# Block products in pairs of token chunks and down products in pairs of output tiles, alternating PSUM banks

## The chip, the cores and the metric

One Trainium2 chip, of which one core runs the whole kernel. The metric is the device time of one execution in microseconds (us); smaller is better. Times of a kernel are medians of several executions; the trace comes from one more, profiled, execution.

## The reference

One inference step of a decoder layer for two groups of tokens that share the weights: 1024 prompt tokens and 8 x 8 sample tokens, model width 1024, all in float32. The layer is

- `x = x + 0.5 * SwiGLU_1(RMSNorm(x))`
- a combined input projection; windowed attention with three dilations (heads A) and a Conformer convolution module (channels B); `x = x + [A | B] @ W_out`
- `x = x + CrossAttention(RMSNorm(x), memory)`
- `x = x + 0.5 * SwiGLU_2(RMSNorm(x))`, and a final RMSNorm

with keys, values and convolution rows returned as new cache entries. The part that this change touches is the feed-forward half step, used twice:

```
def ffn_half_step(x, g, wg, wu, wd):
    h = rmsnorm(x, g)
    return x + 0.5 * ((jax.nn.silu(h @ wg) * (h @ wu)) @ wd)
```

`wg` and `wu` are 1024 x 2816, `wd` is 2816 x 1024. The tokens of both groups stand side by side: 1088 columns.

## The kernel before, in words

Activations are held transposed: model channels on the 128 partitions, tokens along the free dimension. A float32 product is made of three matmuls in the type fp32r: weights and activations are each split into a high and a low part, and the helper `three` (L920 to L922) issues high x high, low x high and high x low into the same PSUM bank. PSUM has eight banks, written `ps[:, bank, ...]`. The 1088 token columns are cut in two ways: into chunks of 384, 384 and 320 columns (`CHUNKS`), or into two halves of 544 (`TH`), each of two chunks of 272 (`CW`).

The hidden width 2816 is worked off in 11 groups of 256. In `ffn` of the tensor block, the first group is done plainly (`plain`): gate and up for two hidden tiles and three chunks, over 8 channel tiles each. The other ten (`REST`) are done by `halved(i)`. It replaces the eight block products of a 2 x 2 by 2 x 2 block matrix product by seven, with sums and differences of blocks as operands: for `w = 0` (gate) and `w = 1` (up) seven products `m = 0` to `6`, each over 4 channel tiles, for both 272-column chunks `c`. So one chunk of one block product is 4 x 3 = 12 matmuls. `product` (L935) issues them for one chunk; chunk 0 comes first, then chunk 1, and each has its own PSUM bank (`one + c`, `two + c` or `three_ + c`) and its own increment of the semaphore `pp`. `hh` and `hl` hold the activations' high and low parts, `th` and `tl` those of the block differences.

The weights come by DMA, issued by SP, into four quarters of `raw`. POOL makes sums and differences of blocks (L835), a high part (L803) and a low part (L805) in a ring of six slots; it waits for a slot by `pp` in steps of two or by `down` in steps of twelve.

ACT copies finished blocks out of PSUM (L1668), applies SiLU (L1673, L1688) and casts the hidden values to their high part (L1678). DVE adds a kept block to a finished one (L2311), multiplies gate and up (L2321) and makes the low part of the hidden values (L2325). The hidden values come in four pieces per group, 0 to 3, each of one hidden tile and one token half, each worked chunk by chunk. Piece 2 is finished after product 5 of `w = 1`, piece 3 after product 6. PE's waits on `up`, `part` and `hid` in `halved` say when it may write into a bank again or read the hidden values.

Then `down` (L958) multiplies the two hidden tiles by the 256 x 1024 slice of `wd`: 8 output tiles x 3 chunks = 24 tiles, six matmuls each (two hidden tiles, three parts), in four banks in turn. DVE adds half of each to `x` (L2271, `residual`) and increments `res`; PE waits before tile `j` until tile `j - 4` has been added. In the first group's `down(0, ...)` DVE makes differences of activation blocks (L2187, L2226, L2242, L2196) beside the residuals, after every fourth, and ACT casts them (L1633); both finish them before their part of `halved(0)`. In the last group of the second feed-forward the tiles go by rows of tokens, `beside_down` transposes finished tokens on PE (L1589) between them, and DVE writes the normalised output (L2820) beside the residuals.

Every engine follows its own list, written out by hand; nothing reorders it.

## Time and profile before

| | |
|---|---|
| time, median of 3 | 2586.61 us (2585.22 to 2592.68) |
| time of the profiled execution | 2590.64 us |
| its span | 2588.6 us |
| mean granted clock of TensorE | 0.99 |
| PE busy | 2487.2 us, 96% |
| PE weight loads busy | 2335.2 us, 90% |
| DVE busy | 1226.5 us, 47% |
| POOL busy | 1160.4 us, 45% |
| ACT busy | 662.6 us, 26% |
| data moved | 224.67 MB, 87 GB/s |

The span is the profiler's, from the first to the last instruction; the time of the execution has 2.0 us around it. PE is TensorE. Its matmuls are pipelined and each is shown longer than the distance to the next one, so the distance between the starts of two matmuls says what one costs. PEld are the weight loads, which run beside the matmuls. What stands in brackets, as `[0.49 <-PE ps L922]`, is the time in which the engine had nothing to run before this row, and what ended it.

### The profile page before, as it was taken

The page shows a single profiled execution, that of the slowest core. Times are in us where ns is not written, and L with a number is a line of the kernel's source. Part 1 is how long each engine was busy: PE and PEld are TensorE (multiplying, and loading weights), DVE is VectorE, ACT ScalarE, POOL GpSimd, SP SyncE. Part 2 cuts the span into 40 slices and gives each one's busy share as a digit, 9 for nine tenths or more (in the row PEclk, how much of TensorE's full clock was granted, in tenths as well). Part 3 has the DMA queues.
Part 4 walks back from the last instruction along what each step waited for, and adds up shares of the span by engine and source line. Part 5 has one row for each costly group of instructions (what it writes and reads, how often), then busy time and mean ns, then how long its engine had stood idle before and what let it go on. Part 6 is the DMA issues. An engine that isn't in the chain of part 4 may idle for free.

```text
span 2588.6 us, 48515 instructions
## 1 busy us (share of the span) xinstructions
PE 2487.2 (96%) x17731; PEld 2335.2 (90%) x17731; DVE 1226.5 (47%) x2562; ACT 662.6 (26%) x1673; POOL 1160.4 (45%) x1068
## 2 busy tenths in 40 slices
PE   7999999999999999989999999889899999999997
PEld 7999999999998899967557999669799999999997
DVE  5653333333335799544433342642963333333335
ACT  4321111111113224266223122331321111111113
POOL 7466666666664222023001220213166666666662
PEclk9999999999999999999999999999999999999999
DMA  7311111111112112155864123641011111111112
GB/s 236 96 42 47 46 46 46 46 46 47 49 49 73 33 53 88 72 161 163 334 245 154 49 76 118 260 173 50 17 46 45 48 45 47 45 46 46 48 49 94
DMA packets 215993, 224.67 MB, mean 87 GB/s; under 512 B 12090, under 2 KB 183670, under 8 KB 211795
## 3 DMA queue, kind: packets, MB, share of 16 engines
q1 hardware_dynamic: 199399, 195.46, 23.3%
q10 hardware_dynamic: 16492, 27.82, 2.9%
q8 instruction: 68, 1.11, 0.2%
q14 instruction: 34, 0.28, 0.0%
HBM read 190.84 MB, written 32.40 MB: 86 GB/s over the span
## 4 chain that ended last, share of the span: by engine, by line
PE 88%; DVE 6%; ACT 2%; DMA 2%; issue 1%; ACTq 0%; DVEq 0%; SPq 0%
PE ps L920 25%; PE ps L921 25%; PE ps L922 25%; PE ps L1427 1%; PE ps L1383 1%; PE ps L1397 1%; PE ps L1302 1%; PE ps L1315 1%; DMA cK<-in_cache_mem_k 1%; PE ps L1493 1%; DVE ps L2187 1%; PE ps L1476 1%; DVE ps L2407 1%; PE ps L1285 1%; DVE hl L2384 0%
## 5 line engine op out<-in xcount | busy, mean ns | idle before, releaser
L920 PE MATMUL ps<-hh,wh 128*128 128x272 f32 (+2 forms) x2528 | 781.8, 309 | 21.0 <-ACT gated L1639 7.0
L921 PE MATMUL ps<-hh,wl 128*128 128x272 f32 (+2 forms) x2528 | 778.3, 308 | 0.0
L922 PE MATMUL ps<-hl,wh 128*128 128x272 f32 (+2 forms) x2528 | 778.1, 308 | 0.0
L805 POOL TENSOR_TENSOR wl<-raw,wh 128x512 fp32r<-128x512 f32 x384 | 496.7, 1293 | 30.8
L920 PEld LDWEIGHTS ps<-hh,wh 128*128 128x128 f32 x2528 | 477.8, 189 | 32.1 <-DVE hl L2152 9.0
L921 PEld LDWEIGHTS ps<-hh,wl 128*128 128x128 f32 x2528 | 477.2, 189 | 0.5
L922 PEld LDWEIGHTS ps<-hl,wh 128*128 128x128 f32 x2528 | 476.6, 189 | 0.0
L803 POOL CAST wh<-raw 128x512 fp32r<-128x512 f32 x384 | 236.1, 615 | 532.1 <-PE ps L922 462.5
L2271 DVE SCALAR_TENSOR_TENSOR x<-ps,x 128x384 f32<-128x384 f32 (+1 forms) x528 | 280.1, 535 | 200.4 <-PE ps L922 198.2
L795 POOL CAST wh<-raw 128x1024 fp32r<-128x1024 f32 x52 | 54.1, 1040 | 701.6 <-PE ps L922 576.0
L920 PE MATMUL ps<-hidh,wh 128*128 128x384 f32 (+1 forms) x1056 | 344.6, 326 | 1.2 <-DVE tl L2196 1.2
L922 PE MATMUL ps<-hidl,wh 128*128 128x384 f32 (+1 forms) x1056 | 344.5, 326 | 0.0
L921 PE MATMUL ps<-hidh,wl 128*128 128x384 f32 (+1 forms) x1056 | 344.1, 326 | 0.0
L920 PE MATMUL ps<-th,wh 128*128 128x272 f32 x960 | 276.3, 288 | 3.0 <-ACT gated L1668 3.0
L921 PE MATMUL ps<-th,wl 128*128 128x272 f32 x960 | 277.2, 289 | 0.0
L922 PE MATMUL ps<-tl,wh 128*128 128x272 f32 x960 | 275.9, 287 | 0.0
L835 POOL TENSOR_TENSOR raw<-raw 128x512 f32<-128x512 f32 x160 | 206.9, 1293 | 0.0
L920 PEld LDWEIGHTS ps<-hidh,wh 128*128 128x128 f32 x1056 | 198.3, 188 | 1.7 <-DVE tl L2196 1.5
L2311 DVE TENSOR_TENSOR ps<-ps,parts 128x272 f32<-128x272 f32 x120 | 53.8, 448 | 306.4 <-PE ps L922 306.4
L921 PEld LDWEIGHTS ps<-hidh,wl 128*128 128x128 f32 x1056 | 198.2, 188 | 0.0
L922 PEld LDWEIGHTS ps<-hidl,wh 128*128 128x128 f32 x1056 | 198.2, 188 | 0.0
L2311 DVE TENSOR_TENSOR gated<-ps,gated 128x272 f32<-128x272 f32 x120 | 53.0, 442 | 300.5 <-PE ps L922 300.5
(274 smaller groups left out, 3320.7 us busy)
## 6 DMA issues: line engine op xcount, KB each, us to landing
raw<-in_ffn_gate SPq DMA_DIRECT2D x88, 256.0 KB, 2.9
raw<-in_ffn_up SPq DMA_DIRECT2D x88, 256.0 KB, 2.9
raw<-in_ffn_down SPq DMA_DIRECT2D x88, 256.0 KB, 2.7
Kw<-in_cache_win_k SPq DMA_DIRECT2D x24, 512.0 KB, 6.1
Vw<-in_cache_win_v SPq DMA_DIRECT2D x24, 512.0 KB
raw<-in_w_in SPq DMA_DIRECT2D x20, 512.0 KB, 3.8
Kw<-in_cache_win_k SPq DMA_DIRECT2D x8, 1024.0 KB, 8.5
Vw<-in_cache_win_v SPq DMA_DIRECT2D x8, 1024.0 KB
```

What stands on the lines that cost most here:

```text
L795: pool.tensor_copy(hi, src).then_inc(w_hi, 1)
L803: pool.tensor_copy(ring_hi(r), quadrant(q)).then_inc(s["whi"], 1)
L805: pool.tensor_tensor(ring_lo(r), quadrant(q), ring_hi(r).bitcast(F32), ALU.subtract).then_inc(s["lo"], 1)
L835: pool.tensor_tensor(out, a, b, op).then_inc(s["mix"], 1)
L920: pe.matmul(out, w_hi_, a_hi, start=first, stop=False, skip_group_check=more)
L921: pe.matmul(out, w_lo_, a_hi, start=False, stop=False, skip_group_check=more)
L922: return pe.matmul(out, w_hi_, a_lo, start=False, stop=last, skip_group_check=more)
L1285: mm = pe.matmul(ps[:, 2 * h + n % 2, far(t):far(t) + near(t)], qs[64 * h:64 * h + 64, 1 - p, t * P:(t + 1) * P], kTp[64 * h:64 * h + 64, ...
L1302: mm = pe.transpose(ps[0:w, b, k * P:(k + 1) * P], Sb[:, n % 2, h, c:c + w], ident[:])
L1315: mm = pe.matmul(ps[:, 6 + n % 2, 64 * h:64 * h + 64], PT[:, n % 2, h, len(cuts) + k, :], vtok[:, p, t + 1 - len(whole) + k, 64 * h:64 * h ...
L2271: dve.scalar_tensor_tensor(out=x[:, d, c0:c0 + n], in0=ps[:, bank(j), 0:n], scalar=0.5, in1=x[:, d, c0:c0 + n], op0=ALU.mult, op1=ALU.add) ...
L2311: dve.tensor_tensor(out(c), ps[:, bank + c, 0:CW], kept(c), ALU.add).then_inc(s["part"], 1)
```

## The change

`product` is taken out. In its place `pair` issues one block product for both chunks: for each channel tile and each of the three parts (high x high, low x high, high x low) first the matmul of chunk 0 into one bank, then that of chunk 1 into the next bank, with the same weights. Both chunks then end with consecutive matmuls, and each still increments `pp`. The waits for chunk 0 and for chunk 1 become one wait for both, ahead of the product. In `down` two output tiles of the same chunk are taken together: their matmuls alternate between the two tiles' banks, with different weights and the same activations, and PE waits ahead of a pair until both banks are free. The number of matmuls, the operands of each, the order in which semaphores are incremented and the lists of the other engines stay as they are.

```diff
--- before.py
+++ after.py
@@ -932,12 +932,6 @@
         def ffn(s, sn, beside_last=None):
             lo, sg, hid, res = s.base["lo"], s.base["sg"], s.base["hid"], s.base["res"]
 
-            def product(out, r, k0, k1, a_hi, a_lo, first, last, more=False):
-                for k in range(k0, k1):
-                    mm = three(out, ring_hi(r)[:, k - k0], ring_lo(r)[:, k - k0], a_hi(k), a_lo(k), first and k == k0,
-                               last and k == k1 - 1, more)
-                return mm
-
             def plain(w, c, f):
                 c0, n = CHUNKS[c]
                 j = 6 * w + 2 * c + f
@@ -956,7 +950,7 @@
                 mm.then_inc(s["gate"], 1)
 
             def down(it, lo_need, hid_need, bank, by_rows, beside=None):
-                for j in range(NC * KT):
+                for j in range(0, NC * KT, 2):
                     if by_rows:
                         c, d = divmod(j, KT)
                     else:
@@ -966,19 +960,37 @@
                         pe.wait_ge(s["lo"], lo_need(d // 4))
                     if d % 4 == 0 and (by_rows or d == 0):
                         pe.wait_ge(s["hid"], hid_need(c))
-                    pe.wait_ge(s["res"], it * (NC * KT) + (res + j + 1))
+                    pe.wait_ge(s["res"], it * (NC * KT) + (res + j + 2))
                     if beside is not None and j == 2:
                         pe.wait_ge(s["hid"], hid_need(NC - 1))
                     for f in range(2):
                         r = 2 + 2 * (d // 4) + f
-                        mm = three(ps[:, bank(j), 0:n], ring_hi(r)[:, d % 4], ring_lo(r)[:, d % 4],
-                                   hidh[:, f, c0:c0 + n], hidl[:, f, c0:c0 + n], f == 0, f == 1)
-                    mm.then_inc(s["down"], 1)
+                        for q, (w_, a_) in enumerate(((ring_hi(r), hidh), (ring_lo(r), hidh), (ring_hi(r), hidl))):
+                            for e in range(2):
+                                mm = pe.matmul(ps[:, bank(j + e), 0:n], w_[:, (d + e) % 4], a_[:, f, c0:c0 + n],
+                                               start=f == 0 and q == 0, stop=f == 1 and q == 2)
+                                if f == 1 and q == 2:
+                                    mm.then_inc(s["down"], 1)
                     if beside is not None:
-                        beside(c, d)
+                        for e in range(2):
+                            beside(c, d + e)
+
+            def pair(first_bank, r, k0, src_hi, src_lo, at, first, more):
+
+                for k in range(k0, k0 + KT // 2):
+                    whi, wlo = ring_hi(r)[:, k - k0], ring_lo(r)[:, k - k0]
+                    kk = k if src_hi is hh else k - k0
+                    start, stop = first and k == k0, k == k0 + KT // 2 - 1
+                    for part_, (w_, a_) in enumerate(((whi, src_hi), (wlo, src_hi), (whi, src_lo))):
+                        for c in range(2):
+                            mm = pe.matmul(ps[:, first_bank + c, 0:CW], w_, a_[:, kk, at + c * CW:at + (c + 1) * CW],
+                                           start=start and part_ == 0, stop=stop and part_ == 2,
+                                           skip_group_check=more)
+                            if stop and part_ == 2:
+                                mm.then_inc(s["pp"], 1)
 
             def halved(i, beside=None):
-                pp, cp, ad = s.base["pp"] + 28, s.base["up"], s.base["part"]
+                cp, ad = s.base["up"], s.base["part"]
                 for w in range(2):
                     one, two, three_ = ((0, 2, 4), (6, 4, 2))[w]
                     for m in range(7):
@@ -988,41 +1000,30 @@
                             pe.wait_ge(s["rstd"], s.base["rstd"] + (24 if m == 1 else 32))
                         if w == 0 and m == 1:
                             pe.wait_ge(s["res"], i * (NC * KT) + (res + 4 + NC * KT))
-                        for c in range(2):
-                            if w == 1 and m == 1:
-                                pe.wait_ge(s["part"], i * 12 + (ad + c + 1))
-                            if w == 1 and m == 3:
-                                pe.wait_ge(s["part"], i * 12 + (ad + 4 + c + 1))
-                            if m == 2:
-                                pe.wait_ge(s["up"], i * 12 + (cp + 6 * w + c + 1))
-                            if m == 4:
-                                pe.wait_ge(s["up"], i * 12 + (cp + 6 * w + 4 + c + 1))
-                            if m == 6:
-                                pe.wait_ge(s["part"], i * 12 + (ad + 6 * w + 2 + c + 1))
-                            x0, x1 = c * CW, (c + 1) * CW
-                            y0, y1 = TH + x0, TH + x1
-                            if m == 0:
-                                mm = product(ps[:, one + c, 0:CW], n % RING, 0, 4, lambda k: hh[:, k, x0:x1],
-                                             lambda k: hl[:, k, x0:x1], True, True)
-                            elif m == 1:
-                                mm = product(ps[:, three_ + c, 0:CW], n % RING, 0, 4, lambda k: th[:, 0, k, x0:x1],
-                                             lambda k: tl[:, 0, k, x0:x1], True, True)
-                            elif m == 2:
-                                mm = product(ps[:, one + c, 0:CW], n % RING, 0, 4, lambda k: th[:, 1, k, x0:x1],
-                                             lambda k: tl[:, 1, k, x0:x1], False, True, True)
-                            elif m == 3:
-                                mm = product(ps[:, two + c, 0:CW], n % RING, 4, 8, lambda k: hh[:, k, x0:x1],
-                                             lambda k: hl[:, k, x0:x1], True, True)
-                            elif m == 4:
-                                mm = product(ps[:, one + c, 0:CW], n % RING, 0, 4, lambda k: hh[:, k, y0:y1],
-                                             lambda k: hl[:, k, y0:y1], False, True, True)
-                            elif m == 5:
-                                mm = product(ps[:, three_ + c, 0:CW], n % RING, 0, 4, lambda k: th[:, 2, k, x0:x1],
-                                             lambda k: tl[:, 2, k, x0:x1], False, True, True)
-                            else:
-                                mm = product(ps[:, one + c, 0:CW], n % RING, 4, 8, lambda k: hh[:, k, y0:y1],
-                                             lambda k: hl[:, k, y0:y1], False, True, True)
-                            mm.then_inc(s["pp"], 1)
+                        if w == 1 and m == 1:
+                            pe.wait_ge(s["part"], i * 12 + (ad + 2))
+                        if w == 1 and m == 3:
+                            pe.wait_ge(s["part"], i * 12 + (ad + 6))
+                        if m == 2:
+                            pe.wait_ge(s["up"], i * 12 + (cp + 6 * w + 2))
+                        if m == 4:
+                            pe.wait_ge(s["up"], i * 12 + (cp + 6 * w + 6))
+                        if m == 6:
+                            pe.wait_ge(s["part"], i * 12 + (ad + 6 * w + 4))
+                        if m == 0:
+                            pair(one, n % RING, 0, hh, hl, 0, True, False)
+                        elif m == 1:
+                            pair(three_, n % RING, 0, th[:, 0], tl[:, 0], 0, True, False)
+                        elif m == 2:
+                            pair(one, n % RING, 0, th[:, 1], tl[:, 1], 0, False, True)
+                        elif m == 3:
+                            pair(two, n % RING, 4, hh, hl, 0, True, False)
+                        elif m == 4:
+                            pair(one, n % RING, 0, hh, hl, TH, False, True)
+                        elif m == 5:
+                            pair(three_, n % RING, 0, th[:, 2], tl[:, 2], 0, False, True)
+                        else:
+                            pair(one, n % RING, 4, hh, hl, TH, False, True)
                 down(i + 1, lambda h: i * NS + (lo + NP + 16 + 2 * h if beside is None else lo + NP + 18),
                      lambda c: i * 8 + (hid + 6 + (6 if c == 0 else 8)),
                      (lambda j: 4 + j % 4) if beside is not None else (lambda j: (4, 5, 2, 3)[j % 4]),
```

## Rows read from the trace of the kernel before

**Rows 1.** The page: busy time by engine; the last chain by line.

```profile
PE 2487.2 (96%) x17731; PEld 2335.2 (90%) x17731; DVE 1226.5 (47%) x2562; ACT 662.6 (26%) x1673; POOL 1160.4 (45%) x1068
...
PE ps L920 25%; PE ps L921 25%; PE ps L922 25%; PE ps L1427 1%; PE ps L1383 1%; PE ps L1397 1%; PE ps L1302 1%; PE ps L1315 1%; DMA cK<-in_cache_mem_k 1%; PE ps L1493 1%; DVE ps L2187 1%; PE ps L1476 1%; DVE ps L2407 1%; PE ps L1285 1%; DVE hl L2384 0%
```

**Rows 2.** A steady stretch: PE busy (matmuls), granted clock, DMA share, GB/s.

```profile
1929.00:1994.00 65.00, 65.00 (x475) 1.00 0.17 49
```

**Rows 3.** Groups by shape, PE: names, shapes, count | busy us, mean ns | idle.

```profile
L920 PE MATMUL ps<-hh,wh 128*128 128x272 f32 x1280 | 367.5, 287 | 0.0
...
L920 PE MATMUL ps<-th,wh 128*128 128x272 f32 x960 | 276.3, 288 | 3.0 <-ACT gated L1668 3.0
...
L920 PE MATMUL ps<-hidh,wh 128*128 128x384 f32 x704 | 235.8, 335 | 1.2 <-DVE tl L2196 1.2
```

**Rows 4.** Timeline of DVE, steady down product: start us, duration us.

```profile
2029.84 0.56 DVE L2271 SCALAR_TENSOR_TENSOR x<-ps,x 128x384 f32<-128x384 f32 x1 [0.58 <-PE ps L922]
...
2037.12 0.56 DVE L2271 SCALAR_TENSOR_TENSOR x<-ps,x 128x384 f32<-128x384 f32 x1 [0.48 <-PE ps L922]
```

**Rows 5.** Timeline of PE: the last down tile, and the next block product's first matmul.

```profile
2039.55 0.31 PE L920 MATMUL ps<-hidh,wh 128*128 128x320 f32 x1
...
2040.43 0.29 PE L920 MATMUL ps<-hh,wh 128*128 128x272 f32 x1
```

**Rows 6.** Timeline of PE: first matmuls of four successive block products (one chunk each).

```profile
2050.98 0.29 PE L920 MATMUL ps<-hh,wh 128*128 128x272 f32 x1
...
2052.49 0.29 PE L920 MATMUL ps<-hh,wh 128*128 128x272 f32 x1
...
2054.01 0.28 PE L920 MATMUL ps<-hh,wh 128*128 128x272 f32 x1
...
2055.49 0.28 PE L920 MATMUL ps<-th,wh 128*128 128x272 f32 x1
```

**Rows 7.** Timeline of DVE: the same sum in two successive groups.

```profile
2006.60 0.45 DVE L2311 TENSOR_TENSOR ps<-ps,parts 128x272 f32<-128x272 f32 x1 [13.10 <-PE ps L922]
...
2072.44 0.45 DVE L2311 TENSOR_TENSOR ps<-ps,parts 128x272 f32<-128x272 f32 x1 [13.10 <-PE ps L922]
```

**Rows 8.** Timeline of DVE in W_out: residuals of successive 384-column products of 24 matmuls.

```profile
1454.86 0.56 DVE L2368 TENSOR_TENSOR x<-ps,x 128x384 f32<-128x384 f32 x1 [2.60 <-PE ps L922]
...
1459.02 0.56 DVE L2368 TENSOR_TENSOR x<-ps,x 128x384 f32<-128x384 f32 x1 [3.20 <-PE ps L922]
```

**Rows 9.** Line L1225: count, min/median/max ns, first to last start us.

```profile
L1225 PEld LDWEIGHTS ps<-ya,ones x24: 187/190/190, 1063.4 to 1070.3; 128*128 128x128 f32 x24
```

**Rows 10.** Timeline of DVE and PE from the last block products to down.

```profile
2014.12 0.45 DVE L2311 TENSOR_TENSOR ps<-ps,parts 128x272 f32<-128x272 f32 x1 [0.49 <-PE ps L922]
2014.48 0.79 DVE L2321 TENSOR_TENSOR ps<-ps,gated 128x272 f32<-128x272 f32 x2
2015.37 0.79 DVE L2325 TENSOR_TENSOR hidl<-ps,hidh 128x272 fp32r<-128x272 f32 x2
...
2016.71 0.33 PE L920 MATMUL ps<-hidh,wh 128*128 128x384 f32 x1
```

**Rows 11.** Timeline of DVE and PE in the first down product.

```profile
1886.65 1.94 DVE L2271 SCALAR_TENSOR_TENSOR x<-ps,x 128x384 f32<-128x384 f32 x4
...
1887.35 0.41 PE L920 MATMUL ps<-hidh,wh 128*128 128x384 f32 x1
...
1890.11 1.48 DVE L2271 SCALAR_TENSOR_TENSOR x<-ps,x 128x384 f32<-128x384 f32 x3
...
1906.98 0.29 PE L920 MATMUL ps<-hh,wh 128*128 128x272 f32 x1
```

**Rows 12.** Timeline of ACT and PE at the first group of `halved`.

```profile
1914.22 1.26 ACT L1668 COPY gated<-ps 128x272 f32<-128x272 f32 x4
...
1914.66 0.39 PE L920 MATMUL ps<-th,wh 128*128 128x272 f32 x1 [1.48 <-ACT gated L1668]
```

**Rows 13.** Timeline of DVE: the last residuals of the kernel.

```profile
2569.53 1.02 DVE L2271 SCALAR_TENSOR_TENSOR x<-ps,x 128x320 f32<-128x320 f32 x2
```

## The prediction

> **What bounds the kernel now.** The page comes first: PE is busy 96% of the span, the others at most 47%, and the chain that ended last spends three quarters of the span on the three lines of `three` [rows 1]. The granted clock is 1.00 in the feed-forward stages [rows 2]. So the first reading is TensorE, at its higher level (2.4 GHz). Busy PE doesn't say why each matmul takes what it takes, so the groups by shape give the counts [rows 3], and the order of time gives the distance from one start to the next, which is the real price. Down tiles of six 384-column matmuls follow each other at 1.04 us (2029.84 to 2037.12, seven tiles in 7.28 us) [rows 4], 173.3 ns a matmul; a tile of six 320-column ones takes 0.88 us (2039.55 to 2040.43), 146.7 ns [rows 5]. The difference, 26.6 ns for 64 columns, is 0.416 ns a column; what is left is a fixed part of 13.3 ns a matmul. Block products of twelve 272-column matmuls take 1.48 to 1.52 us, on average (2055.49 - 2050.98) / 36 = 125.3 ns [rows 6]: 113.2 ns of columns and 12.1 ns fixed. Steady blocks repeat every 65.84 us (2006.60 to 2072.44) [rows 7]; 336 x 125.3 ns + 96 x 173.3 ns + 48 x 146.7 ns = 65.8 us. Nothing is left for stalls. DVE, ACT and POOL wait for PE there, not PE for them.
>
> So the change can gain only from the fixed part, and can lose wherever the new order makes PE wait.
>
> **Part 1: the bank alternates from matmul to matmul.** It touches 6720 block matmuls (2 feed-forwards, 10 repeats, 336: the 960 + 1280 of one line, times three) and 3168 down matmuls ((704 with 384 columns and, for the third chunk, half as many with 320) x 3) [rows 3]. Count, columns and arithmetic stay. If the fixed part were the price of two consecutive matmuls into one bank, one gap without it would stand at each bank switch that exists today. A down product switches after 6 matmuls, a W_out product after 24, with the same 384 columns. The 24 take 1459.02 - 1454.86 = 4.16 us, 173.3 ns each [rows 8]; the 6 take 1.04 us, 173.3 ns each [rows 4]. A saving of 13.3 ns per switch would make the average of the short product 1.7 ns smaller (13.3 x (1/6 - 1/24)), 10 ns a tile, 0.07 us over the seven tiles. They show nothing of it. What the 272-column products do vary with is the columns read: the second half's last chunk takes 1.48 us (2054.01 to 2055.49), the first half's second chunk 1.51 (2050.98 to 2052.49) and the second half's first 1.52 (2052.49 to 2054.01) [rows 6]. That points to the reading side. I take 0 for this part. The bounds: all 6720 products of a pair at the best of these rates (1.48/12 = 123.3 ns) give -15 us, at the worst (1.52/12 = 126.7 ns) +8 us, since the alternating chunks change the sequence of addresses; and if the whole fixed part went, 6720 x 12.1 + 3168 x 13.3 ns = -123 us.
>
> The Trainium skill ("TensorE: Matmul & The Clock Gate", Back-to-back issue gap) gives N/2.4 + 2.5 ns for a warm matmul. This trace disagrees: 173.3 ns stands where the rule has 162.5, and 125.3 where it has 115.8. Were the new order to restore the rule, an estimate by that page is 6720 x 9.5 + 3168 x 10.8 ns, some 98 us less; it lies inside the rival below, which is worked out from rows.
>
> **Part 2: same weights twice in succession.** In `pair` both chunks use one weight tile before the next. Today's totals have 17731 loads for 17731 matmuls, and the LayerNorm sums, whose stationary operand is `ones` throughout, have 24 loads for 24 passes [rows 1, 9]. So I expect 17731 loads again, and 0. The bound, if half the block loads vanished with their fixed part, is 3360 x 12.1 ns = -41 us.
>
> **Part 3: both chunks end together.** The evacuation of chunk 0 used to run under chunk 1's 1.5 us. Now both finish 0.125 us apart, and the next user of the bank has one product pair (3.01 us) left instead of 4.5. Copies and sums are short: two ACT copies at 0.31 us pitch [rows 12] or two DVE sums at 0.36 us (2014.12 to 2014.48 [rows 10]). The tightest case is hidden piece 2, which down waits for. Now: the last matmul of product 5 is over when DVE adds at 2014.12, then two multiplies (2014.48), two ACT casts, two subtractions (2015.37 with 0.79), end 2016.16; down's first matmul starts at 2016.71 [rows 10]. A wake-up takes 0.14 us (residual 0 starts at 1886.65 and takes 0.56 us, so it is over at 1887.21; PE starts at 1887.35 [rows 11]), so the margin is 0.41 us. Afterwards the sum of chunk 0 comes 0.125 us ahead of 2014.12 and that of chunk 1 0.36 us behind it; multiplies at 2014.72 instead of 2014.48: +0.24 us. Margin 0.17 us, no stall. The other case, +0.36 us per extra DVE start with no overlap of the casts (another 0.39 us), would be 0.75 us, and is a rival. POOL and SP are not touched: their waits count complete pairs (`pp` in twos, `down` in twelves), which are reached at the same moment.
>
> **Part 4: down in pairs.** A pair needs the residuals of the pair two back. In the repeats DVE takes 0.56 us a tile against 1.04 us of PE [rows 4]: 2.08 us for a pair against 1.04 of DVE, no stall. Not so in the first down product, where DVE first finishes other work and then makes differences beside the residuals. Residual 0 starts at 1886.65, and PE's tile 4 starts right behind its end, at 1887.35 [rows 11]. I stepped through the 24 tiles with 1.04 and 0.88 us a tile on PE, 0.48 and 0.44 us pitch for a residual, and other DVE work after every fourth: 1.6 us the first time (1888.59 to 1890.11 [rows 11]), 1.85 later, once 2.25. One by one, this ends at 1906.84; the trace has the next product's first matmul at 1906.98 [rows 11]. In pairs, PE waits 0.57 us at tile 4 (for residual 1), 0.34 at tile 12 and 0.19 at tile 20, and DVE's last difference comes 1.15 us later. That chain goes on through ACT: its first block copies start at 1914.22 behind the last cast, and PE waits 1.48 us for the first [rows 12]. Now PE needs two, 0.31 us apart (1.26 / 4). So +1.46 us per feed-forward, +2.9 us for both. Bounds: 0 (a shorter DVE list) and twice that.
>
> At the end of the first feed-forward the norm waits for the last residual, now behind one more: +0.3 us. In the last down product, which runs beside the output transposes, DVE has residuals and outputs without a gap, and its last residuals run from 2569.53 to 2570.55 [rows 13]; pair (2,0), (2,1) gives it its first tile 0.88 us later, and the output of token tile 0 stands between residuals that come in twos. Stepped through, the last residual ends near 2571.6 instead of 2570.55: +1.1 us, all of it in the tail.
>
> The Trainium skill ("Perfetto Trace Analysis", Matmuls) has independent groups rotate through banks so that one group's evacuation overlaps the next group's matmuls; pairing halves that rotation. By that rule this change costs overlap; the rows above price it at the 4 us of the sum.
>
> **Sum.** 0 + 0 + 0 + 2.9 + 0.3 + 1.1 = +4.3 us. The profiled execution took 2590.64 us (span 2588.6 and 2.0 around it), 4.0 above the median of 2586.61. On it the sum is 2595; on the median, which is what will be compared, 2591. Without the rivals its range is 2585 to 2598.
>
> **Rivals.** (1) *The fixed part goes or shrinks with alternation or with repeated weights.* For it: it is the only thing in the matmul stream above the column rate. Against it: the rows under part 1. Whole: 2591 - 123 = 2468; with repeated weights alone: 2550. Chance 0.12.
> (2) *Reading order.* The new sequence of moving addresses shifts the 272-column gap within its seen spread. For it: 1.48 against 1.52 us for identical work. To 2576 at best, 2599 at worst; chance 0.07 for a gain that counts and 0.06 for a loss.
> (3) *Evacuation becomes the bound, slower.* One mechanism: the chain of hidden piece 2, in each of 20 blocks. It decides when it grows by more than 0.41 us. If the second chunk's cast and subtraction don't overlap (0.75 us), each block stalls 0.34 us, 7 us in all, and the multiplies of piece 3 push the first residuals too; 2598 to 2602. For it: margin only 0.17 us after my own sum. Against it: casts and multiplies overlap in the rows of now. Chance 0.15.
> The forecast as summed: 0.60, of which some 0.03 lies beyond +0.3%.
>
> **How the numbers follow.** A change within 0.3% (7.8 us) is what a measurement of this kernel can't tell from none; it is said once. Faster: rival 1 and the better half of 2, 0.12 + 0.07, and 0.01 of the forecast for the unforeseen: 0.20. Slower: 0.06 + 0.15 + 0.03 = 0.24, less 0.02 where rival 3 stays under 7.8 us: 0.22. Same: 0.58. The range, 2576 to 2602, leaves out rival 1 and a little at either end.
>
> **What would show it.** Gap between starts of block matmuls: 125 to 126 ns if right, near 115 if rival 1. Loads still 17731. Sum, multiply and cast of both chunks close together, and down's first matmul without idle time in front; idle there in each block is rival 3. In the first down product, idle before the third pair, near 0.6 us. If the time falls by more than 1%, the step that failed is part 1 or 2; if it rises by more than 0.5%, part 3.

## The result, and the profile after

Fifteen executions of each kernel on one chip: before 2588.82 us (2585.22 to 2603.21), after 2594.30 us (2588.36 to 2599.46). The ratio is 1.0023, with a 95% interval of 1.0014 to 1.0033: the change costs 5.9 us (3.6 to 8.5). The forecast was +4.3 us, within 0.3%; the direction and the place were right, two of the terms were not. The profiled execution of after took 2591.56 us with a span of 2589.4, only 0.8 us more than the span of before. That is not the difference to explain: one execution differs from the next by several us in stages that the change doesn't touch (below), so the stretches around the change are compared one by one.

Lines of the page of after: the engines; the chain by engine; the costliest groups (block products, down product, the block products that read differences, and weight loads), with the names, shapes and count, then busy us, mean ns and idle time ahead with what ended most of it.

```profile
PE 2490.9 (96%) x17731; PEld 2339.3 (90%) x17731; DVE 1192.4 (46%) x2562; ACT 642.6 (25%) x1673; POOL 1159.0 (45%) x1068
...
PE 89%; DVE 6%; ACT 2%; issue 1%; DMA 1%; ACTq 0%; DVEq 0%; SPq 0%
...
L986 PE MATMUL ps<-hh,wh 128*128 128x272 f32 x1280 | 264.9, 288 | 0.0
...
L970 PE MATMUL ps<-hidh,wh 128*128 128x384 f32 (+1 forms) x1056 | 259.5, 326 | 0.4 <-DVE x L2272 0.4
...
L986 PE MATMUL ps<-th,wh 128*128 128x272 f32 x960 | 200.2, 290 | 3.6 <-ACT gated L1669 3.6
...
L986 PEld LDWEIGHTS ps<-hh,wh 128*128 128x128 f32 x1280 | 202.1, 188 | 0.0
```

PE is still the chain and has as many loads as before [rows 1]: 17731. The reader is to see two things that are not as they were. The loads of the line that now uses each weight tile twice in a row are still 1280, one for each matmul. And the idle time in front of the block products has gone from 3.0 us [rows 3] to 3.6 us, all of it behind ACT's copies.

Next the steady groups, in the timeline of DVE and then of PE. Columns are start, duration, engine, line, operation, and in brackets the idle time ahead and what ended it; x2 or x4 at the end are so many instructions drawn as one.

```profile
2007.80 0.80 DVE L2312 TENSOR_TENSOR ps<-ps,parts 128x272 f32<-128x272 f32 x2 [14.29 <-PE ps L986]
...
2013.81 0.80 DVE L2312 TENSOR_TENSOR ps<-ps,parts 128x272 f32<-128x272 f32 x2 [0.44 <-PE ps L986]
2014.52 0.79 DVE L2322 TENSOR_TENSOR ps<-ps,gated 128x272 f32<-128x272 f32 x2
2015.40 0.79 DVE L2326 TENSOR_TENSOR hidl<-ps,hidh 128x272 fp32r<-128x272 f32 x2
...
2020.73 1.02 DVE L2272 SCALAR_TENSOR_TENSOR x<-ps,x 128x384 f32<-128x384 f32 x2 [1.06 <-PE ps L970]
2022.81 1.02 DVE L2272 SCALAR_TENSOR_TENSOR x<-ps,x 128x384 f32<-128x384 f32 x2 [1.06 <-PE ps L970]
...
2073.67 0.80 DVE L2312 TENSOR_TENSOR ps<-ps,parts 128x272 f32<-128x272 f32 x2 [14.29 <-PE ps L986]
```

```profile
2016.29 0.41 PE L986 MATMUL ps<-hl,wh 128*128 128x272 f32 x2
2016.53 0.52 PE L970 MATMUL ps<-hidh,wh 128*128 128x384 f32 x2
```

The period is 65.87 us (2007.80 to 2073.67) where it was 65.84 [rows 7]. Hidden piece 2 runs through its sum, multiply and low part in the same way as before [rows 10]: from the first sum to the end of the low part 2.38 us now (2013.81 to 2016.19). Down's first matmul starts at 2016.53, 0.34 us after that end and 0.24 us behind the start of the last block pair, which is the distance of one pair, so there is no idle time. A pair of down tiles takes 2.08 us (2020.73 to 2022.81), twice the 1.04 of [rows 4]. So in 18 of the 20 groups nothing waits, and the loss must lie at the ends.

The table gives the distances between the starts of the first matmuls of neighbouring stretches in the profiled executions ("tail" runs to the end of the last instruction):

```
us                              before    after    difference
feed-forward 1: first down       23.72    23.91    +0.19
                first group      43.88    45.76    +1.88
                nine groups     592.62   592.86    +0.24   (9 x 65.847, 9 x 65.873)
                last down        24.51    24.75    +0.24
feed-forward 2: first down       24.03    24.70    +0.67
                first group      43.88    45.78    +1.90
                nine groups     592.62   592.89    +0.27
                tail             45.11    45.87    +0.76
sum                                               +6.15
not touched: before PE's first
             matmul             13.61    12.91    -0.70
             from it to the
             first down        123.58   121.50    -2.08
             attention, mixing 1061.03  1058.48    -2.55
```

"First group" is the 336 block matmuls of the first `halved`, without its down product; "nine groups" start with that down product and end where the last one starts. The sum, +6.15, agrees with the +5.9 that was timed. The last two of the untouched stretches took 121.5 to 123.6 us and 1057.9 to 1063.9 us over all the kernels below, in no relation to their edits, and that hides the difference between single spans.

3.8 of the 6.15 us lie in the two first groups. Here is the second of them, in the timelines of ACT and PE of after:

```profile
1911.88 0.39 ACT L1634 CAST hh<-ps 128x272 fp32r<-128x272 f32 x1 [2.31 <-DVE ps L2243]
1912.16 1.26 ACT L1669 COPY gated<-ps 128x272 f32<-128x272 f32 x4
```

```profile
1912.90 0.52 PE L986 MATMUL ps<-th,wh 128*128 128x272 f32 x2 [1.82 <-ACT gated L1669]
...
1914.01 0.61 PE L986 MATMUL ps<-th,wl 128*128 128x272 f32 x2
...
1914.88 0.66 PE L986 MATMUL ps<-th,wh 128*128 128x272 f32 x2
...
1916.69 0.66 PE L986 MATMUL ps<-th,wl 128*128 128x272 f32 x2
...
1917.54 0.41 PE L986 MATMUL ps<-hh,wh 128*128 128x272 f32 x2
1917.79 0.41 PE L986 MATMUL ps<-hh,wl 128*128 128x272 f32 x2
```

Before, PE started 0.44 us behind ACT's first copy (1914.22 and 1914.66 [rows 12]); now it needs two copies and starts 0.74 us behind it (1912.16 and 1912.90), and its idle time is 1.82 us, where it was 1.48. That step is the forecast's. What it didn't foresee comes 1.1 us later: from 1914.01 to 1917.54 eight pairs take 3.53 us, 0.44 each, and then a pair takes 0.25 again. The windows of PE say why; columns are the stretch, its length, PE busy with the matmuls, the granted clock, the DMA share and GB/s.

```profile
1915.00:1917.00 2.00, 2.00 (x11) 0.50 0.02 6
...
1919.00:1921.00 2.00, 2.00 (x18) 1.00 0.00 0
```

The granted clock is 0.50 there, the lower of TensorE's two levels (1.2 GHz), after it had been 1.00 up to the wait, and a matmul of 272 columns takes 0.226 us (eight in the 1.81 us from 1914.88 to 1916.69). Eight pairs cost 3.53 - 8 x 0.251 = 1.5 us more. In the first feed-forward of the same execution it is the same:

```profile
164.00:168.00 4.00, 2.18 (x12) 0.80 0.55 158
168.00:172.00 4.00, 4.00 (x28) 0.77 0.12 37
172.00:176.00 4.00, 4.00 (x34) 1.00 0.00 0
```

In the kernel before the windows around the same waits all have 1.00, as this one, which holds the second:

```profile
1912.00:1916.00 4.00, 2.52 (x20) 1.00 0.46 133
```

The timeline of PE in the first down product of the second feed-forward shows the paired wait on the residuals:

```profile
1885.03 0.59 PE L970 MATMUL ps<-hidh,wh 128*128 128x384 f32 x2 [0.39 <-DVE x L2272]
...
1892.51 0.46 PE L970 MATMUL ps<-hidl,wh 128*128 128x320 f32 x2
1892.95 0.58 PE L970 MATMUL ps<-hidh,wh 128*128 128x384 f32 x2
```

At tile 4 the wait is shown; at tile 12 it is to be read from the starts: 0.44 us behind the pair ahead, where a pair of 320 columns takes 0.29.

At the end of the kernel the last residuals are late. These are the first matmuls of the last down product, of before and of after, and DVE's last residuals of after:

```profile
2543.49 0.33 PE L920 MATMUL ps<-hidh,wh 128*128 128x384 f32 x1
```

```profile
2543.55 0.58 PE L970 MATMUL ps<-hidh,wh 128*128 128x384 f32 x2
```

```profile
2570.47 0.89 DVE L2272 SCALAR_TENSOR_TENSOR x<-ps,x 128x320 f32<-128x320 f32 x2
```

The last residual ends 27.81 us behind the start of the last down product (2571.36 - 2543.55); before it was 27.06 (2570.55 [rows 13] - 2543.49): +0.75, which is the tail's +0.76.

### The profile page after: what moved, and what is told of

It is laid out like the page before. It is cut to its first block, busy times and chain, and to the rows that moved or that the text cites. A ratio compares the mean times of both kernels' runs of the same rounds, so it can differ in the third digit from the quotient of the medians.

```text
span 2589.4 us, 48155 instructions
## 1 busy us (share of the span) xinstructions
PE 2490.9 (96%) x17731; PEld 2339.3 (90%) x17731; DVE 1192.4 (46%) x2562; ACT 642.6 (25%) x1673; POOL 1159.0 (45%) x1068
## 4 chain that ended last, share of the span: by engine, by line
PE 89%; DVE 6%; ACT 2%; issue 1%; DMA 1%; ACTq 0%; DVEq 0%; SPq 0%
PE ps L986 32%; PE ps L970 20%; PE ps L920 8%; PE ps L922 7%; PE ps L921 7%; PE ps L1384 2%; PE ps L1428 1%; PE ps L1398 1%; PE ps L1303 1%; PE ps L1316 1%; DMA cK<-in_cache_mem_k 1%; PE ps L1494 1%; PE ps L1477 1%; DVE ps L2188 1%; DVE ps L2408 1%
## 5 line engine op out<-in xcount | busy, mean ns | idle before, releaser
L920 PE MATMUL ps<-hh,wh 128*128 128x384 f32 (+1 forms) x1248 | 414.8, 332 | 19.4 <-ACT gated L1640 7.1
L922 PE MATMUL ps<-hl,wh 128*128 128x384 f32 (+1 forms) x1248 | 410.1, 329 | 0.0
L921 PE MATMUL ps<-hh,wl 128*128 128x384 f32 (+1 forms) x1248 | 409.8, 328 | 0.0
L986 PE MATMUL ps<-hh,wl 128*128 128x272 f32 x1280 | 264.9, 288 | 0.0
L986 PE MATMUL ps<-hh,wh 128*128 128x272 f32 x1280 | 264.9, 288 | 0.0
L986 PE MATMUL ps<-hl,wh 128*128 128x272 f32 x1280 | 264.6, 288 | 0.0
L970 PE MATMUL ps<-hidh,wh 128*128 128x384 f32 (+1 forms) x1056 | 259.5, 326 | 0.4 <-DVE x L2272 0.4
L970 PE MATMUL ps<-hidh,wl 128*128 128x384 f32 (+1 forms) x1056 | 259.3, 326 | 0.0
L970 PE MATMUL ps<-hidl,wh 128*128 128x384 f32 (+1 forms) x1056 | 259.0, 326 | 0.0
L986 PE MATMUL ps<-th,wl 128*128 128x272 f32 x960 | 199.6, 289 | 0.0
```

Of the source, the lines that this page charges most:

```text
L920: pe.matmul(out, w_hi_, a_hi, start=first, stop=False, skip_group_check=more)
L921: pe.matmul(out, w_lo_, a_hi, start=False, stop=False, skip_group_check=more)
L922: return pe.matmul(out, w_hi_, a_lo, start=False, stop=last, skip_group_check=more)
L970: mm = pe.matmul(ps[:, bank(j + e), 0:n], w_[:, (d + e) % 4], a_[:, f, c0:c0 + n], start=f == 0 and q == 0, stop=f == 1 and q == 2)
L986: mm = pe.matmul(ps[:, first_bank + c, 0:CW], w_, a_[:, kk, at + c * CW:at + (c + 1) * CW], start=start and part_ == 0, stop=stop and part ...
```

## Experiments

The theory of the start: the loss comes from the first down product and the first group, where the residuals and the copies decide when PE goes on, and half of it is the clock that falls behind the longer wait (this half came with the profiles of e1 to e4; the expectations count with it from e8 on). Its rival is a cost spread over all groups: alternating banks, repeated weights, or the order in which the moving operand is read. All ratios are against the kernel before in the same comparison (2586.68 us, 30 runs, for the first four; 2587.25 us, 23 runs, for the others).

### Either half of the change alone

`e1_blocks_paired` keeps `pair` and takes `down` back:

```diff
-                for j in range(0, NC * KT, 2):
+                for j in range(NC * KT):
...
-                    pe.wait_ge(s["res"], it * (NC * KT) + (res + j + 2))
+                    pe.wait_ge(s["res"], it * (NC * KT) + (res + j + 1))
...
-                        for q, (w_, a_) in enumerate(((ring_hi(r), hidh), (ring_lo(r), hidh), (ring_hi(r), hidl))):
+                        mm = three(ps[:, bank(j), 0:n], ring_hi(r)[:, d % 4], ring_lo(r)[:, d % 4],
+                                   hidh[:, f, c0:c0 + n], hidl[:, f, c0:c0 + n], f == 0, f == 1)
```

> Block products in pairs, down tiles one by one as before. Theory A (the alternating order itself costs nothing; the change loses only where PE waits longer): DVE's list in the first down product is not delayed, so only the second ACT copy (0.31 us, twice) and the 0.04 us a steady group that the changed kernel's block products took more (42.17 against 42.13 us, 18 groups) remain: +1.4 us over before, about 4 us below the changed kernel. Rival B (what the change costs is spread evenly over the reordered matmuls): 6720 of 9888 of them are here, so two thirds of the 5.9 us, +4. Rival C (chunks that finish together make PE wait in each group): +3 or more, with idle time of PE before down in each group.

`e2_down_paired` is the kernel before with only the new `down` (the same lines the other way round).

> Down tiles in pairs, block products chunk by chunk as before. Theory A: PE waits at tiles 4, 12 and 20 of the first down product, DVE's differences come 1.1 us later and with them the first group's third block product (1.1 to 1.6 us, twice); +0.2 us at the end of the first feed-forward, +0.7 us in the last down product; steady down products 23.70 instead of 23.72 us: +3 to +4 us over before. Rival B (spread evenly): 3168 of 9888, one third, +2 us.

Measured: e1 2593.09 us (8 runs), ratio 1.0020 [1.0009, 1.0030]; e2 2591.55 us (11), 1.0020 [1.0009, 1.0030]. By time the two can't be told from each other or from the whole change, so the stretches have to do it (differences to before, us):

```
                     first down   first group    nine groups    last down   tail    sum
e1_blocks_paired     0.00, 0.00   +1.86, +0.32   +0.24, +0.27   -0.02       +0.78   +3.5
e2_down_paired      +0.22, +0.68  +0.05, +0.04    0.00, 0.00    +0.25       +1.44   +2.7
after               +0.19, +0.67  +1.88, +1.90   +0.24, +0.27   +0.24       +0.76   +6.15
```

The first down product belongs to the paired `down` alone, the nine groups and the first group to the paired blocks alone. And the two first groups of e1 show the two parts of the latter apart. They wait alike, but only one of them is followed by a lower clock. First the timeline of PE in e1, in the first and in the second feed-forward, then its windows behind the first wait and behind the second:

```profile
167.53 0.52 PE L982 MATMUL ps<-th,wh 128*128 128x272 f32 x2 [1.78 <-ACT gated L1665]
```

```profile
1917.68 0.52 PE L982 MATMUL ps<-th,wh 128*128 128x272 f32 x2 [1.77 <-ACT gated L1665]
```

```profile
168.00:172.00 4.00, 4.00 (x22) 0.57 0.24 66
172.00:176.00 4.00, 4.00 (x34) 1.00 0.00 0
```

```profile
1920.00:1924.00 4.00, 4.00 (x34) 1.00 0.00 0
```

So the second copy costs 0.3 us, and the clock 1.5 us when it falls. The expectation for e1 counted only the former and was too low for that reason. Its time alone, +5.2 us (2.3 to 7.8), would fit the +4 of rival B, the evenly spread cost, as well; the stretches refute that rival, since the 18 steady groups together hold 0.5 us. For e2 +3 to +4 us were expected. The stretches give +2.7, of which 0.7 is the lower clock in the tail (below): the two first down products cost 0.2 and 0.7 us where 1.1 to 1.6 each stood.

The tails need one more look, because e1 has the old `down` there and still loses 0.78 us. The last 32 transposes of the kernel, by the timelines of PE, first after, then e1, then e2:

```profile
2575.58 3.68 PE L1590 MATMUL ps<-ident,x 128*128 128x128 f32 x32 [0.97 <-DVE ytok L2821]
```

```profile
2578.13 5.29 PE L1586 MATMUL ps<-ident,x 128*128 128x128 f32 x32 [0.97 <-DVE ytok L2817]
```

```profile
2578.57 6.62 PE L1593 MATMUL ps<-ident,x 128*128 128x128 f32 x32 [0.97 <-DVE ytok L2824]
```

And the window of PE in e2 that the last of them lies in:

```profile
2580.00:2584.00 4.00, 4.00 (x21) 0.50 0.47 190
```

The longer ones are again the lower clock, behind the short waits on DVE between the transposes; before, after, e5, e6 and e7 have 3.7 us for the same work, e3, e4 and e8 5.1 to 5.4. It comes and goes between executions, in one of four with an unpaired last `down` and in four of six with a paired one, too few to say whether the pairing has a part in it. The tail's price of the paired `down` is therefore read from the executions without it: +0.76 (after) and +0.79 (e6). The start of these 32 transposes, which the clock behind them can't move, says the same: it comes 31.2 to 31.3 us behind the start of the last down product in before, e1, e5 and e7, and 32.0 to 32.1 us in the six kernels with the paired one.

### The first down product and the first group as before, the rest paired

```diff
-            down(0, lambda h: lo + 10 + 2 * h, lambda c: hid + 2 * c + 2, lambda j: 4 + j % 4, False)
+            down_single(0, lambda h: lo + 10 + 2 * h, lambda c: hid + 2 * c + 2, lambda j: 4 + j % 4, False)
+            halved_single(0)
             if beside_last is None:
-                with pe.Fori(0, REST) as i:
+                with pe.Fori(1, REST) as i:
                     halved(i)
```

`down_single` and `halved_single` are the old functions, the latter with a paired down product behind its block products.

> The changed kernel, but the first down product and the block products of the first halved group are one by one as before, in both feed-forwards. Theory A: the waits of the first group go back to before (first halved group 43.88 us instead of 45.76, first down product without the added waits); left are 17 or 18 steady groups at +0.03 us and the last down products, +1.0 us: +1.5 us over before, 4 to 4.5 below the changed kernel. Rival B: 9 tenths of the reordered matmuls are still there, +5.3 us, no more than 0.6 us below the changed kernel.

Measured: 2592.23 us (11 runs), ratio 1.0017 [1.0008, 1.0026]. By the stretches: first down 0.00 and -0.03, first group +0.07 and +0.06, nine groups +0.25 and +0.28, last down +0.24, tail +1.48 (with the lower clock, its 32 transposes took 5.06 us), sum +2.4. Expected were +1.5 over before; without the tail's lower clock (0.7 us) 1.6 of the 2.35 are left. The loss at the start is gone, as the theory of the start has it, and the nine groups are unchanged at 65.873 us each, so nothing of the 3.8 us was spread over groups. The time itself fell less than the stretches say (+4.4 us, interval 2.1 to 6.7, against +2.4): by the ratios e3 is 1.5 us below the whole change, where 4 to 4.5 were expected and rival B allowed 0.6. The interval holds both, and this run's time alone would not have decided.

### The weight tiles of chunk 1 in another order

```diff
-                    for part_, (w_, a_) in enumerate(((whi, src_hi), (wlo, src_hi), (whi, src_lo))):
+                    parts_ = ((whi, src_hi), (wlo, src_hi), (whi, src_lo))
+                    for part_ in range(3):
                         for c in range(2):
+                            w_, a_ = parts_[(0, 1, 2)[part_] if c == 0 else (1, 0, 2)[part_]] if part_ < 2 else parts_[2]
```

For the first two parts chunk 1 takes them in the other order; banks still alternate with every matmul. The six matmuls of a channel tile now load high, low, low, high, high, high, where after has high, high, low, low, high, high. So the expectation below is right that only one pair in three has the same weights in both chunks, but a weight tile still comes directly after itself in three of six cases, as often as in after. This run is no test of repeated weights.

> The changed kernel, but in each block product the two chunks use different weight tiles (high and low in turn) for the first four of six matmuls, so the banks still alternate while only one pair in three repeats its weights; the same sums in another order. Theory A: neither the bank nor a repeated weight tile has a part in the gap between matmuls: 125 to 126 ns a block matmul, 17731 weight loads, time as the changed kernel within 2 us. Rival D (alternation costs what repetition gives back, the two cancel): the gap grows by some ns, 6720 x 2 ns = 13 us for each 2 ns.

Measured: 2593.02 us (10 runs), ratio 1.0025 [1.0016, 1.0035], the same as the whole change, and each of the eight stretches but the tail is within 0.03 us of after's. Its page, and the window behind the wait of the second feed-forward:

```profile
PE 2493.0 (96%) x17731; PEld 2343.4 (90%) x17731; DVE 1192.4 (46%) x2562; ACT 643.3 (25%) x1673; POOL 1160.6 (45%) x1068
```

```profile
1915.00:1917.00 2.00, 2.00 (x11) 0.50 0.44 127
```

Which chunk reads which weight tile makes no difference, and the clock falls here too, in both first groups. What separates the bank from the repeated weights is the down product. Its paired form alternates banks and never repeats a weight tile, and from its first matmul to the next block product the steady stretch of 144 matmuls takes 23.718 us in e2 and 23.717 in before, and 23.704 in both after and e1, whose `down` is unpaired. So alternation alone costs nothing; the 0.013 us go with the paired block products on either side. Repeated weights are in the block products of e6 and not in those of e5, next.

### The start column of the moving operand

The nine groups lose 0.026 us each. The kernel before reads 272-column chunks that start at columns 0, 272, 544 and 816 (in the block differences at 0 and 272). To separate the start column from the order, `e5_starts_single` (from before) and `e6_starts_paired` (from after) use chosen starts, with the same remainder by 64 for both chunks. The `32 * (k % 2)` keeps the remainder the same for all channel tiles of the block differences, whose rows of 544 columns are 32 more than a multiple of 64. Both kernels so read other columns than the layer needs, and the values of their feed-forwards are not the layer's; the matmuls, their sizes and all waits stay. The edit as it stands in e6 (in e5 `product` gets the same starts):

```diff
+            def start_of(w, m, c, k):
+                ph = ((0, 0, 16, 16, 32, 32, 48), (8, 48, 8, 24, 40, 24, 56))[w][m]
+                if m in (1, 2, 5):
+                    return 128 * c + (ph + 32 * (k % 2)) % 64
+                return 256 * c + (448 if m in (4, 6) else 0) + ph
...
-                            mm = pe.matmul(ps[:, first_bank + c, 0:CW], w_, a_[:, kk, at + c * CW:at + (c + 1) * CW],
+                            x0 = start_of(w, m, c, k)
+                            mm = pe.matmul(ps[:, first_bank + c, 0:CW], w_, a_[:, kk, x0:x0 + CW],
```

> The kernel before, with the moving operands of the block products read from other columns than they should be (so the feed-forward's values are others; nothing else is left out): each product starts at a chosen column, with a remainder by 64 of 0, 16, 32, 48 in the gate products and of 8, 24, 40, 56 in the up products, the same for both chunks and all channel tiles. Theory A (the 12 ns above the column rate and their spread come from the reading of the moving operand): the gap follows the start column, 123 to 127 ns by remainder, whichever bank is written. Rival: it doesn't follow it, and all 14 products show 125 to 126 ns or keep the pattern of before.

> The same start columns in the changed kernel (same remark on the values). Theory A: with equal remainders in both chunks the paired products show the same gap as the chunk-wise ones with that remainder, within 0.5 ns, since neither bank nor repeated weights matter. Rival (the pairing itself adds something per matmul): they are slower at every remainder by a like amount, 0.5 ns or more.

Measured, one execution each: 2584.84 and 2596.07 us. Single executions can't be compared as times; the distances within them can. The groups (timeline of DVE, the sum of rows 7, first e5, then e6) have one period, 65.81 us:

```profile
2001.10 0.45 DVE L2316 TENSOR_TENSOR ps<-ps,parts 128x272 f32<-128x272 f32 x1 [13.02 <-PE ps L922]
...
2066.91 0.45 DVE L2316 TENSOR_TENSOR ps<-ps,parts 128x272 f32<-128x272 f32 x1 [13.02 <-PE ps L922]
```

```profile
2012.86 0.80 DVE L2319 TENSOR_TENSOR ps<-ps,parts 128x272 f32<-128x272 f32 x2 [14.19 <-PE ps L993]
...
2078.67 0.80 DVE L2319 TENSOR_TENSOR ps<-ps,parts 128x272 f32<-128x272 f32 x2 [14.19 <-PE ps L993]
```

The mean distance from matmul to matmul within a block product, as the median over the groups (first start of a product to first start of the next, by 24):

```
ns, w = 0        m0      m1      m2      m3      m4      m5      m6
before         125.79  125.58  125.29  125.79  124.88  125.46  124.83
after          126.08  125.50  125.29  126.46  125.12  125.00  125.00
e5 (single)    125.17  125.25  126.67  126.67  126.62  126.67  123.50
e6 (paired)    125.17  125.25  126.67  126.67  126.62  126.67  123.50
```

e5 and e6 agree to the last digit in all seven, and as exactly in the seven of `w = 1`. So with equal remainders alternating banks and using one weight tile twice together change nothing, and as alternation alone changes nothing in `down`, neither does the repeated weight tile. One matmul of 272 columns takes 123.4 to 126.7 ns by where it starts: 125.2 at remainder 0, 126.7 at 16 and 32, 123.5 at 40 and 48. That is the spread; the 10 to 13.5 ns above the 113.2 ns of columns are there at every remainder tried, and no run shows what they are. After differs from before because its chunks start 272 columns apart, remainder 16, and the two are now read in turn: m3 +0.67, m0 +0.29, m5 -0.46. Over the 336 matmuls that is +0.04 us; the stretch of the down product gives 0.01 back (23.717 to 23.704), and +0.026 is left. The sum, 0.51 us in 18 groups, is small but is the whole of the steady loss.

e6 is again a case in which the clock fell behind one of its two long waits: first group +0.33 and +1.83 us. Over the eight kernels that have the wait:

```
idle time of PE before the third block product     first groups   clock fell behind it
1.48 to 1.57 us  (before, e2, e3, e5)                    8               0
1.77 to 1.85 us  (after, e1, e4, e6)                     8               6
```

In e1 the two waits are equal (1.78 and 1.77 us) and the clock fell behind one of them only, so the length alone doesn't decide. The Trainium skill ("TensorE: Matmul & The Clock Gate", Part 1) calls the number of slow matmuls at a start variable from run to run of one kernel. What varied here is whether the clock fell; where it did, the number of slow matmuls was 15 or 16 each of the six times.

### Taking away the wait

The wait of the first group is for ACT, whose copies of block product 0 stand in its list behind its last casts of block differences, though they need none of them. `e7_copy_first_before` (from before) and `e8_copy_first_after` (from after) move the copies ahead of the last two casts, in the first group alone:

```diff
-            for q in range(24, 32):
-                turned(q)
-
-            def halved(i):
+            def halved(i, first=False):
...
+                    for q in range(24, 30):
+                        turned(q)
+                    keep(0, 0, gated, 0)
+                    for q in range(30, 32):
+                        turned(q)
...
-            with act.Fori(0, REST) as i:
+            halved(0, True)
+            with act.Fori(1, REST) as i:
```

> The kernel before; ACT makes the first group's first block copies ahead of its last two casts of differences instead of behind them. Theory A: PE's wait at the third block product (1.5 us by the list of waits, a gap of 1.77 us) is for those copies only, so it goes, in both feed-forwards: first group 42.2 instead of 43.9 us, 3 us less in all, if the sixth and seventh block products don't wait then. Rival: the last differences (needed by the fourth product) are late next, and 1 us or less is won.

> The same move of ACT's copies in the changed kernel. Theory A: the changed kernel loses in its first groups by a wait of 2.1 us instead of 1.77 and by the half clock that follows it (some 15 matmuls at 227 ns instead of 125, 1.5 us); without the wait there is no half clock, both first groups take 42.2 us instead of 45.8, 7 us less than the changed kernel and 1 us or so below before. Rival (the half clock comes from the pairing or from chance, not from that wait): matmuls at 227 ns remain in one or both first groups and at most 4 us are won.

Measured: e7 2586.14 us (11 runs), ratio 0.9993 [0.9984, 1.0002]; e8 2588.28 us (12 runs), ratio 1.0003 [0.9994, 1.0011]. The timeline of ACT and the windows of PE in e8, first feed-forward:

```profile
164.42 0.68 ACT L1666 COPY gated<-ps 128x272 f32<-128x272 f32 x2 [0.41 <-PE ps L986]
165.63 0.39 ACT L1634 CAST hh<-ps 128x272 fp32r<-128x272 f32 x1 [0.54 <-DVE ps L2248]
```

```profile
164.00:168.00 4.00, 4.00 (x35) 1.00 0.44 123
168.00:172.00 4.00, 4.00 (x34) 1.00 0.48 141
```

PE doesn't wait and the clock stays at 1.00. The first groups take 42.17 us in e8 and 42.13 in e7, against 45.8 in after and 43.88 in before: 3.6 us less in each feed-forward of the one and 1.75 in the other. Of the change's 0.23%, 0.03% is left, with an interval that holds 1. But before has the wait too, and loses 1.75 us by it, so e8 against before mixes two changes. The price of pairing without the wait is e8 against e7: +2.85 us by the stretches (0.4 of it the lower clock in the tail of e8) and 0.10%, some 2.6 us, by the two ratios, where it is 6.15 and 5.9 us with the wait. This is the test of the largest term: with the wait both of its prices go, the 0.3 us and the 1.5 us of clock. For e7 the stretches say -3.5 us and the timing -1.8 (-4.1 to +0.5); no gain over the kernel before can be claimed from these runs. For e8 1 us or so below before was expected; the stretches say -0.7 and the timing +0.8 (-1.6 to +2.8).

## Why the prediction was right in sign and size, and where it was not

The sum was +4.3 us; the stretches give +6.15 and the timing +5.9. By its own steps:

- **Part 1, alternating banks: 0.** Right: e5 and e6 are the same in every product. Rival 1, that the fixed part goes or shrinks, is refuted; block matmuls stand 125.0 to 126.5 ns apart in after.
- **Part 2, repeated weights: 0.** Right: 17731 loads, and e6 with repeats is as e5 without; alternation alone is nothing by `down` (23.718 us in e2, 23.717 in before). Two figures of parts 1 and 2 are a little off: by 0.416 ns a column the fixed part of a 384-column matmul is 13.6 ns, not 13.3, and from 125.3 ns the bounds of the reading order are -13 and +9 us, not -15 and +8. No term of the sum hangs on them.
- **Part 1's reading order**, rival 2, bounded at -15 to +8 us and taken at 0: it is real, and +0.5 us in all.
- **Part 3, both chunks end together: 0 in the steady groups.** Right: down starts without idle time, and rival 3 does not occur. The low part is over 0.34 us before down starts; less the wake-up of 0.14 that is a margin of 0.20 us, where the forecast had 0.17.
- **Part 4, the residuals of a pair in the first down product.** The step that failed in size is "+1.46 us per feed-forward", of which 1.15 is the delay of DVE's last difference. The forecast stepped through the second feed-forward and took the result for both. There it was near: PE waits 0.98 us in all (24.70 less the 23.72 of a product without waits), where the three waits of the forecast add up to 1.10. But 0.31 of it was there before (24.03), and ACT's first copy comes 31.98 us behind the start of the product (1912.16 less 1880.18) instead of 31.26 (1914.22 [rows 12] less 1882.96): 0.7 us later, not 1.15. In the first feed-forward DVE is far earlier. The first residual of before starts 1.61 us behind the product's first matmul there, and in the second 3.69 us (1886.65 [rows 11] less 1882.96). The rows are, of before, PE at the start of the first and of the second such product and DVE's first residual in the first; then, of after, PE at the start of the second:

```profile
137.19 0.34 PE L920 MATMUL ps<-hidh,wh 128*128 128x384 f32 x1
```

```profile
1882.96 0.44 PE L920 MATMUL ps<-hidh,wh 128*128 128x384 f32 x1 [1.20 <-DVE tl L2196]
```

```profile
138.80 0.55 DVE L2271 SCALAR_TENSOR_TENSOR x<-ps,x 128x384 f32<-128x384 f32 x1
```

```profile
1880.18 0.62 PE L970 MATMUL ps<-hidh,wh 128*128 128x384 f32 x2
```

With 2 us more of slack PE waits 0.19 us there in after, and nothing in before. Both together: 0.86 us where 2.3 stood.
- **Part 4, the second copy of ACT: 0.31 us.** Right: +0.33 (idle time 1.48 to 1.82).
- **What the step left out is the clock.** The forecast took the price of PE's wait to be its length. Behind the longer wait 16 matmuls ran at the lower level, 1.5 us in each feed-forward, 3.1 in all: half of the loss. The two errors have opposite signs, and that the total of +4.3 comes so near to the measured +5.9 is in that part luck. By length alone the step would be 0.86 + 0.66 = 1.5 us, half of the predicted 2.9; with the clock it is 4.6.
- **End of the first feed-forward:** 0.3 predicted, 0.24 measured. **Tail:** 1.1 predicted, 0.76 measured; the last residual comes 0.75 us later, not 1.1.

Together: 0.86 + 0.66 + 3.1 + 0.5 + 0.24 + 0.76 = 6.1 us. What stays open: the timed differences of e1 to e3 are 1.7 to 2.5 us above the sums of their stretches. The intervals hold this, and the stretches are of one execution each, in which the clock may fall or not; how often it falls behind the waits in the executions that were only timed was not seen. Their mean granted clock is known, a median of 0.990 for before, 0.989 for e2, 0.988 for e3, 0.987 for e8 and e4, and 0.986 for after, e1 and e7. It is lower than before's in each of them, also in e7, which has no such wait, so it doesn't tell in which stage the rest is lost. Whether the 0.3 us by which the wait is longer is what lets the clock fall, or the order of the matmuls behind it, was not tried by itself: a kernel with unpaired products and the longer wait is missing.

## What to carry to other kernels

A wait of the bound engine is priced by its length and by what the clock does behind it: look at the granted clock in narrow windows behind each wait, above all where the wait grows. Rotating banks matmul by matmul and reusing a weight tile at once brought nothing here. Finishing two chunks, or two output tiles, together lengthened the path only where another engine's list had no slack: in the first down product, in the first group and at the end. The cheaper remedy is in that list: a copy that stood behind work it didn't need cost 1.75 us in each feed-forward before, and 3.6 after.

## What the runs showed of the hardware

- A 272-column fp32r matmul takes 123.4 to 126.7 ns by the remainder of its moving operand's start column by 64, the same with or without alternating banks and with or without a fresh weight tile. A whole steady group, 336 block and 144 down matmuls, took 65.813 us with the chosen starts (e5) against 65.847 in before, both unpaired. The remainders tried are the multiples of 8.
- At the lower clock the fixed part of a matmul is not seen: 0.226 us for 272 columns is 0.83 ns a column, twice the 0.416 ns of the higher level with nothing over it.
- Idle times of 1.77 to 1.85 us in an otherwise full PE were followed by a granted clock of 0.50 in six of eight cases, those of 1.48 to 1.57 in none of eight; the former all stand in kernels with paired block products, the latter in front of unpaired ones, so the two can't be told apart. The lower clock also appears in the last transposes of some executions (5.1 to 6.6 us for 32 instead of 3.7; e1, e2, e3, e4 and e8).
